# Last quarter of the down projection with the tokens as stationary operand, and the final normalisation along rows

## The reference, cut to what matters

```python
def rmsnorm(x, w):
    xf = x.astype(jnp.float32)
    y = xf * lax.rsqrt(jnp.mean(xf * xf, axis=-1, keepdims=True) + RMS_EPS)
    return (y * w.astype(jnp.float32)).astype(x.dtype)
...
    x = x + mix @ w_out
    hn = rmsnorm(x, ln2_w)
    x = x + jnp.square(jax.nn.relu(hn @ w_up)) @ w_down
```

## Time and profile before

| | |
|---|---|
| median of 3 runs | 700.5 us (700.15 to 701.1) |
| the profiled execution | 700.22 us, span 698.5 us |
| busy: PE, PEld | 683.0 us (98%), 640.9 us (92%) |
| busy: DVE, POOL, ACT | 443.9 us, 323.3 us, 296.3 us |
| DMA | 100.41 MB, mean 144 GB/s |

### The profile page before, as it was taken

One profiled execution on the slowest core, in us unless ns is written; L12 is line 12 of the kernel. 1 busy time (PEld: TensorE's weight loads), 2 busy tenths in 40 slices (PEclk: granted clock), 3 DMA queues, 4 the chain that ended last, 5 costly groups with the idle time before them and its releaser, 6 DMA issues.

```text
span 698.5 us, 15196 instructions
## 1 busy us (share of the span) xinstructions
PE 683.0 (98%) x5563; PEld 640.9 (92%) x5563; DVE 443.9 (64%) x890; ACT 296.3 (42%) x568; POOL 323.3 (46%) x233
## 2 busy tenths in 40 slices
PE   6999999999999999999999999999999999999996
PEld 6999988888777787999999999999999999999996
DVE  4488889886342456537798685857657576575134
ACT  6532735465342233246555443443433534334222
POOL 6839999823131434247327617053260623507431
PEclk9999999999999999999999999999999999999999
DMA  7936999844477888633112323332232331413103
GB/s 246 302 119 168 266 283 276 269 141 119 144 248 205 254 269 183 146 106 122 61 39 84 121 64 126 115 111 78 89 125 80 120 98 66 139 62 121 61 1 123
DMA packets 88633, 100.41 MB, mean 144 GB/s; under 512 B 5374, under 2 KB 64338, under 8 KB 88570
## 3 DMA queue, kind: packets, MB, share of 16 engines
q1 hardware_dynamic: 74566, 92.91, 42.7%
q10 hardware_dynamic: 14004, 6.67, 4.2%
HBM read 92.92 MB, written 6.64 MB: 143 GB/s over the span
## 4 chain that ended last, share of the span: by engine, by line
PE 79%; DVE 9%; POOL 5%; issue 3%; ACT 2%; DMA 1%; SPq 0%; DVEq 0%; POOLq 0%; ACTq 0%
PE acc L915 6%; PE acc L916 6%; PE acc L917 6%; PE acc L1419 5%; PE acc L1420 5%; PE acc L1418 5%; POOL prod L1973 4%; PE scr L1419 3%; PE scr L1420 3%; PE scr L1418 3%; PE scr L1385 3%; PE scr L1384 3%; PE scr L1386 3%; PE acc L1384 3%; PE acc L1386 3%
## 5 line engine op out<-in xcount | busy, mean ns | idle before, releaser
L915 PE MATMUL acc<-act_hi,w_hi 128*128 128x256 f32 (+1 forms) x416 | 120.6, 290 | 0.8 <-DVE zT L2504 0.8
L2020 POOL TENSOR_TENSOR h_lo<-relu,h_hi 128x520 fp32r<-128x520 f32 x32 | 44.2, 1385 | 165.0 <-ACT h_hi L1805 164.6
L916 PE MATMUL acc<-act_lo,w_hi 128*128 128x256 f32 (+1 forms) x416 | 117.3, 282 | 0.0
L917 PE MATMUL acc<-act_hi,w_lo 128*128 128x256 f32 (+1 forms) x416 | 117.2, 282 | 0.0
L1504 POOL TENSOR_TENSOR w_lo<-raw,w_hi 128x1024 fp32r<-128x1024 f32 x24 | 57.2, 2388 | 96.5 <-ACT w_hi L1497 94.1
L1973 POOL TENSOR_TENSOR prod<-kv,Qb 128x1024 f32<-128x1024 f32 x32 | 85.7, 2712 | 15.9 <-DVE S L2206 10.2
L915 PEld LDWEIGHTS acc<-act_hi,w_hi 128*128 128x128 f32 x416 | 78.4, 188 | 3.6 <-issue 2.3
L916 PEld LDWEIGHTS acc<-act_lo,w_hi 128*128 128x128 f32 x416 | 78.4, 189 | 0.5
L917 PEld LDWEIGHTS acc<-act_hi,w_lo 128*128 128x128 f32 x416 | 78.2, 188 | 0.0
L2523 DVE TENSOR_TENSOR xT<-acc,xT 128x260 f32<-128x260 f32 x64 | 26.6, 424 | 48.4 <-PE acc L1420 48.4
L2504 DVE TENSOR_TENSOR zT<-acc,rstd 128x264 f32<-128x264 f32 (+1 forms) x56 | 23.5, 421 | 44.5 <-PE acc L917 41.0
(11 more groups left out here) (422 smaller groups left out, 2302.2 us busy)
## 6 DMA issues: line engine op xcount, KB each, us to landing
kv<-in_cache_k_dram SPq DMA_DIRECT2D x64, 256.0 KB, 3.4
kv<-in_cache_v_dram SPq DMA_DIRECT2D x64, 256.0 KB, 3.0
raw<-in_w_up_dram SPq DMA_DIRECT2D x16, 1024.0 KB, 5.4
raw_d<-in_w_down_dram SPq DMA_DIRECT2D x12, 1024.0 KB, 5.1
raw<-in_w_in_dram SPq DMA_DIRECT2D x14, 512.0 KB, 6.1
raw<-in_w_in_dram SPq DMA_DIRECT2D x7, 1024.0 KB, 7.2
x_tok<-in_x_prompt_dram SPq DMA_DIRECT2D x8, 512.0 KB, 5.4
raw<-in_w_out_dram SPq DMA_DIRECT2D x4, 1024.0 KB, 7.6
```

The costliest lines, as they stand in the source:

```text
L915: pe.matmul(out, W_HI[home(g)][:, k, :], hi[k][:, cols], start=(n == 0), stop=False)
L916: pe.matmul(out, W_HI[home(g)][:, k, :], lo[k][:, cols], start=False, stop=False)
L917: mm = pe.matmul(out, W_LO[home(g)][:, k, :], hi[k][:, cols], start=False, stop=(n == KT - 1))
L2020: pool.tensor_tensor(h_lo[:, t, :], relu2[:, t % 2, :], h_hi[:, t, :].bitcast(F32), ALU.subtract).then_inc(s_hs_lo, 1)
```

## The change

The last quarter is turned round. 128 prompt tokens (`h_hi`, `h_lo`) are the stationary operand, 512 columns of w_down are moving, and the result has tokens on its partitions. There are 16 blocks j: token tile i = j % 4, output half c = j // 4 % 2, hidden eighth d = j // 8. A block is 4 k-tiles of 3 matmuls, 192 matmuls in all. Results go to `y_out` (token rows), no longer to `xT`: for j < 8 ACT copies the block (L1921) and DVE adds the transposed `xT` (`y_to_tok`, 8 groups of 4 transposes, now all of them early in the phase; L2793); for j >= 8 DVE adds the block from PSUM (L2801).

The 8 sample tokens are no longer columns of these matmuls. `down_samples`, once per eighth, multiplies them (`h_smp`, padded to 32 columns) by the unsplit weights in `raw_d`, in float32, spread over four column groups of the array; in the first call eight more products add `xT`. `sample_sums` adds the groups up.

The final normalisation follows each token tile: ACT squares 512 channels and accumulates along the row (L1928), DVE adds the two halves' sums, POOL takes the power, DVE finishes channels 512 to 1023, ACT channels 0 to 511, which POOL has multiplied by lnf_w (L2136). The sample rows go through the same steps, on DVE between token tiles 2 and 3. In the last phase a raw slot's third load also waits for the first `down_samples`. The stores go out in the order 0, 1, samples, 2, 3.

```diff
             counts = [2] * 6 + [1] * 2
         else:
-            counts = [2] * 6 + [0] * 2
+            counts = [2, 2, 0, 0, 0, 0, 2, 2, 2, 2] + [0] * 6
...
+                    if kind == "last" and q >= 2:
+                        sp.wait_ge(s_smp_down, 1)
...
-                        src = w_down[0, e * EIGHTH:, q * 2 * P:(q + 1) * 2 * P]
-                        dst = raw[:, r % 2, :, :]
+                        src = w_down[0, (e + q // 2) * EIGHTH:(e + q // 2 + 1) * EIGHTH,
+                                     (q % 2) * 4 * P:(q % 2 + 1) * 4 * P]
+                        dst = raw_d[:, r % 2, :, :]
...
-            for i in range(NT + 1):
-                sp.wait_ge(s_y_half, i + 1)
-                evacuated(sp, "yt", i, 1)
+            for i in (0, 1, NT, 2, 3):
                 if i < NT:
+                    sp.wait_ge(s_y_half, i + 1)
+                    sp.wait_ge(s_y_fin, i + 1)
                     sp.dma_start(y_prompt[0, i * P:(i + 1) * P, :], y_out[:, i, :]).then_inc(s_y_stored, 16)
                 else:
+                    sp.wait_ge(s_y_fin_s, 1)
...
+            def down_tokens(j):
+
+                i, c, n = j % 4, j // 4 % 2, LAST + 4 * (j // 4)
+                out = acc[:, j % 3, :]
+                if j == 8:
+                    pe.wait_ge(s_hs_lo, 32)
+                bank_free("last", 6, j, 0)
+                for k in range(4):
+                    if i == 0:
+                        lo_made(pe, n + k)
+                    t, tokens = 4 * (j // 8) + k, slice(i * P, (i + 1) * P)
+                    w = flat(u_hi[(n + k) % RING]), flat(u_lo[(n + k) % RING])
+                    pe.matmul(out, h_hi[:, t, tokens], w[0], start=(k == 0), stop=False)
+                    pe.matmul(out, h_lo[:, t, tokens], w[0], start=False, stop=False)
+                    mm = pe.matmul(out, h_hi[:, t, tokens], w[1], start=False, stop=(k == 3))
...
+            def down_samples(d):
...
+                for k in range(4):
+                    for c in range(2):
+                        r = UNITS[LAST + 8 * d + 4 * c][3]
+                        pe.wait_ge(raw_in[r % 2], mlp_raw_target(r))
+                        g = 32 * (2 * c + k % 2)
+                        mm = pe.matmul(acc[g:g + 32, 3, :], h_smp[:, 4 * d + k, :], raw_d[:, r % 2, k, :],
+                                       start=(d == 0 and k < 2), stop=(d == 1 and k >= 2))
...
             def down_last():
...
+                for j in range(16):
+                    down_tokens(j)
...
+                    if 1 <= j < 9:
+                        y_to_tok((j - 1) % 4, (j - 1) // 4)
+                    if j in (3, 11):
+                        down_samples(j // 8)
+                    if j == 13:
+                        sample_sums()
...
+            def down_last():
+
+                squares(7, 3)
+                for j in range(16):
+                    for u in PREPARE["last", 6, j]:
+                        unit_hi(u)
+                    i, c = j % 4, j // 4 % 2
+                    if j < 8:
+                        block_done(act, j)
+                        act.activation(y_half(j), acc[:, j % 3, :], ACT.Copy).then_inc(s_dn_evac, 1)
+                        continue
+                    act.wait_ge(s_dn_evac, 16 * 6 + j + 1)
+                    if j >= 10:
+                        act.wait_ge(s_y_sq, j - 9)
+                    if j == 15:
+                        act.wait_ge(s_y_sq_s, 1)
+                    act.activation(y_junk[:, j % 2, 0:512], y_half(j), ACT.Square, scale=D ** -0.5,
+                                   accum_out=y_sq[:, c, i:i + 1]).then_inc(s_y_sq, 1)
...
+                    if j >= 12:
+                        act.wait_ge(s_y_pow, i + 1)
+                        act.wait_ge(s_y_pre, i + 1)
+                        x = y_out[:, i, 0:512]
+                        act.activation(x, x, ACT.Copy, scale=y_ms[:, i:i + 1]).then_inc(s_y_half, 1)
+                    if j == 14:
...
+                        act.activation(y_junk[0:NS, 1, :], y_out[0:NS, NT, :], ACT.Square, scale=D ** -0.5,
+                                       accum_out=y_sq[0:NS, 0, NT:NT + 1]).then_inc(s_y_sq_s, 1)
...
+            for i in range(NT):
+                pool.wait_ge(s_y_sq, i + 1)
+                x = y_out[:, i, 0:512]
+                pool.tensor_tensor(x, x, lnf_b[:, 0:512], ALU.mult).then_inc(s_y_pre, 1)
+            for i in range(NT):
+                if i == NT - 1:
+                    pool.wait_ge(s_y_ms_s, 1)
+                    rsqrt(y_ms[0:NS, NT:NT + 1], NS, 1).then_inc(s_y_pow_s, 1)
+                pool.wait_ge(s_y_ms_ok, i + 1)
+                rsqrt(y_ms[:, i:i + 1], P, 1).then_inc(s_y_pow, 1)
...
+                for j in range(8, 16):
+                    i, c = j % 4, j // 4 % 2
+                    block_done(dve, j)
+                    evacuated(dve, "yt", i, c)
+                    dve.tensor_tensor(y_half(j), acc[:, j % 3, :], y_half(j), ALU.add).then_inc(s_dn_evac, 1)
...
+                    dve.wait_ge(s_y_eps, i + 1)
+                    dve.wait_ge(s_y_sq, 4 + i + 1)
+                    dve.tensor_tensor(y_ms[:, i:i + 1], y_sq[:, 0, i:i + 1], y_sq[:, 1, i:i + 1], ALU.add)\
+                       .then_inc(s_y_ms_ok, 1)
+                    dve.wait_ge(s_y_pow, i + 1)
+                    dve.scalar_tensor_tensor(out=y_half(j), in0=y_half(j), scalar=y_ms[:, i:i + 1],
+                                             in1=lnf_b[:, 512:D], op0=ALU.mult, op1=ALU.mult).then_inc(s_y_fin, 1)
+                    if i == 1:
+                        out = full(dve, "ys")
+                        for g in range(4):
+                            ins = dve.tensor_copy(y_out[0:NS, NT, 256 * g:256 * g + 256],
+                                                  out[32 * g:32 * g + NS, 0:256]).then_inc(s_y_smp, 1)
+                    if i == 2:
+                        dve.wait_ge(s_y_sq_s, 1)
...
```

More of the change, by code:

```diff
@@ L254, in plan @@
                 job(*name, i)
-    for i in range(NT + 1):
[L256 to L260, removed]
+    for c in range(2):
+        for i in range(NT):
+            job("yt", i, c)
+    job("ys")
     return tasks, jobs
@@ L373, in banks @@
         else:
-            for j in range(16):
-                b = j % 4 if kind == "last" else BANK_ORDER[(6 + j) % 8]
+            for j in range(17 if kind == "last" else 16):
+                b = (j % 3 if j < 16 else 3) if kind == "last" else BANK_ORDER[(6 + j) % 8]
                 use[kind, e, j] = b, last.get(b)
@@ L1333, in _, with y_to_tok @@
                         task(*name)
-            def y_to_tok(i, part):
-                n = P if i < NT else NS
-                out = open_job(pe, "yt", i, part)
+            def y_to_tok(i, c):
+                out = open_job(pe, "yt", i, c)
                 for j in range(4):
[L1340 to L1352, removed]
+                    mm = pe.transpose(out[:, j * P:(j + 1) * P], xT[:, 4 * c + j, i * P:(i + 1) * P], ident[:, :])
                 done(mm)
@@ L1434, in down @@
                                       None if k < 3 else s_u_done if half else s_dn0)
-            def down_last():
[L1438 to L1461, removed]
@@ new lines, in sample_sums @@
+            def sample_sums():
+                pe.wait_ge(s_y_pick, 2)
+                pe.wait_ge(s_y_grp, 1)
+                out = open_job(pe, "ys")
+                for c in range(2):
+                    for q in range(2):
+                        g = 32 * (2 * c + q)
+                        mm = pe.matmul(out[g:g + NS, 0:256], y_pick[:, c, :], y_grp[:, 256 * q:256 * q + 256],
+                                       start=True, stop=True)
+                done(mm)
+            def down_last():
+                for j in range(16):
+                    down_tokens(j)
+                    if j == 1:
+                        pe.wait_ge(s_dn_evac, 16 * 6)
+                        pe.wait_ge(s_c_ok, 14 * 8 - 6)
+                        pe.wait_ge(s_p_copy, 2 * 7)
+                    if 1 <= j < 9:
[4 more added lines that the diff above has]
+                        sample_sums()
@@ L1479, in _ @@
                 phase(what, e)
[L1480 to L1486, removed]
         def weight_hi(act, g, r_slot, target):
@@ L1876, in phase @@
                     up(e, i)
-                else:
[L1878 to L1884, removed]
-                act.activation(y_out[0:n, i, 0:512], y_out[0:n, i, 0:512], ACT.Copy, scale=y_ms[0:n, i:i + 1])\
-                   .then_inc(s_y_half, 1)
+                elif kind == "down":
+                    down(e, i)
+                else:
+                    down_last()
             for s in range(N_HALVES):
@@ L1906, in _ @@
                 phase(what, e)
-            for i in range(NT + 1):
-                y_scale(i)
             act.wait_ge(s_v_out0, 32)
@@ L2043, in phase @@
             def phase(kind, e, i=0):
-                for step in range(14 if kind == "up" else 8):
```

(11 more changed lines are left out.)

149 lines of the change are left out of this document (86 added, 63 removed).

## The result

| | before | after |
|---|---|---|
| median of 6 runs each | 700.37 us (700.15 to 701.1) | 707.2 us (706.61 to 707.79) |
| ratio, 95% interval | | 1.0097 [1.0087, 1.0107] |
| span of the profiled execution | 698.5 | 705.6 |
| start of the phase's first matmul | 640.09 | 640.88 |
| stretch 1, to the start T of the last matmul | 48.9 | 53.2 |

T is the start of the phase's last matmul, as in the prediction. The profiled execution of the changed kernel took 707.74 us. The changed kernel is slower by 6.8 us, where 4.6 were forecast; the time lies in the range. But the two stretches aren't what was forecast: stretch 1 grew by 4.3 (forecast 1.3), stretch 2 by 2.0 (forecast 3.3).

The account below looks back on a forecast made before the run. PE's matmul count times spacing was taken to bound the phase, then a chain across engines after T; +1.3 and +3.3 make +4.6 on 700.22, so 704.8, median 705.1; own range 703.4 to 706.8, stated 702.5 to 707.4.

Parts of the forecast that it names:

- stretch 1: Last phase, first matmul's start to the last one's start T: 48.9 us before, forecast 50.2, so 1.3 longer.
- stretch 2: From T to the end of the span, the tail: 9.5 us before, forecast 12.8, so 3.3 longer.
- Rival 1: Tail: DVE does not pile up, last add starts at T + 0.4, end at T + 7.4; 699.7 us, chance 0.14.
- eight float32 products in four column groups, 1.0 us from start to start: PE in stretch 1: price of one down_samples call; with 0.1 for the switch, 2.2 us for two calls.
- the other two terms: PE in stretch 1: eight products with `xT` in four groups, 0.3 us, and sample_sums, 0.3 us.
- Rival 3: Stretch 1: 512-column matmuls near the bare 2.4 GHz rate, 0.216 us each; 702.9 us, chance 0.05.
- Rival 4: Sample products on PE: column groups do not overlap, adding 4.8 us; 709.9 us, chance 0.03.
- rival 2: PE stalls 1 to 2 us at block 8 for weight unit 10 or 11; 706 to 707 us, chance 0.10.
- The store: End of the tail: last store's issue to the span's end, taken as 3.7 us, lower bound 3.0.
- The add of block 15: DVE in the tail: the last block's add starts at T + 5.8 instead of T + 0.4, behind the samples.
- the four copies: DVE after tile 1: four 8x256 sample copies out of PSUM, about 0.35 us each back to back, 1.4 us.
- the samples' chain: Tail after tile 2: ACT's sample square, DVE, POOL and DVE's 8x1024 multiply ahead of the last add; 3.9 us.

Follow-up runs that it names:

- experiment 5: Changed kernel with block 15's add moved in DVE's order to right behind tile 2's multiply, ahead of the samples' mean and multiply: 706.37 us, ratio 1.0084.
- experiment 6: Changed kernel with the tail's order on DVE, ACT and POOL rewritten and the samples' sums on PE put earlier, no work left out: 702.28 us, ratio 1.0026.
- experiment 1: Changed kernel without the samples' work in the last phase, y_sample stored as zeros: 697.5 us, ratio 0.995.
- Experiment 2: Changed kernel without the products of k-tiles 2 and 3 in both down_samples calls (8 of 16): 705.47 us, ratio 1.0067.
- experiment 3: Changed kernel with sample products in two column groups instead of four, sample_sums and ACT's copy gone, DVE copying 2 x 512 columns: 710.51 us, ratio 1.0141.
- experiment 4: Changed kernel with each 512-wide matmul of the 16 blocks split into two of 256 columns: 707.75 us, ratio 1.010.

## Why the prediction was right, and where it was wrong

**The direction and its mechanism held.** What was removed, the 9.5 us behind T, is gone as a whole, and what took its place is, as said, DVE waiting in its own order with the last add behind the samples. Of the points of the changed profile that were named, these came true: the spacing of 0.23, the last add right behind the samples' multiply (T + 5.33), ACT's sample square between the scalings of tiles 2 and 3, the last store alone, no idle PE ahead of block 8; the 50.2 and 12.8 us of the two stretches did not. Experiments 5 and 6 show the cause by moving only the order. Rival 1 (DVE does not pile up) is what experiment 6 produces; there the order that it needs had to be written.

**The step that failed: "eight float32 products in four column groups, 1.0 us from start to start".** The row was counted as products where it counts two records for each. The loop behind the earlier trace rows in the kernel before issues four products a time; eight records to four products should have been seen by dividing. Measured: from the end of block 3's transposes (653.38) to one spacing ahead of 656.09, 2.5 us with the `xT` products; 2.1 for the second call and 0.75 for the sums, each with the longer first spacing behind it: 5.3 where 2.8 stood in the sum (5.4 by experiment 1). The same doubling is in the other two terms: L1491 has 16 records for eight products and takes 0.55, where 0.3 were forecast. Experiment 2 shows the size (1.84 us for half of the products), experiment 3 excludes the other explanation.

**The rest of stretch 1.** 191 spacings of 0.2325 are 44.4, forecast 44.0: +0.4. Transposes 3.5 as forecast. 44.4 + 3.5 + 5.3 = 53.2. Rival 3, 0.216 per matmul, would have made them 41.3; neither this trace nor experiment 4 agrees. The Trainium skill (TensorE: Matmul & The Clock Gate, Back-to-back issue gap) gives this 0.216 as the gap of a single matmul with 512 columns; for a stream of weight loads and matmuls the same section has 0.131, which this stream, at 0.2325, is further from still. Rival 4 is excluded by experiment 3, rival 2 by the unchanged spacing around block 8.

**The tail was forecast 1.3 too long.** The store 3.0 where 3.7 was taken, though 3.0 was the lower bound: -0.7. Its bytes start to move 0.83 after the issue (the prediction had 0.4 for this as a bound that no run shows), move for 1.44, and the span ends 0.8 later. The add of block 15 at T + 5.33, not 5.8: block 12's add came 0.5 earlier against T, since the sums stand between it and T and take more, and the chains are shorter, 3.04 for a tile and not 3.11 (-0.2 in all); the four copies took 1.8, not 1.4, 0.45 each (+0.4); the samples' chain 3.8, forecast 3.9. From add to issue 3.2, forecast 3.3.

**So the two errors partly cancel**: +3.0 in stretch 1, -1.3 in the tail. That the time fell within the range is in part luck. It lies outside the 703.4 to 706.8 that the forecast's own terms gave, and inside the stated 702.5 to 707.4 only because this was widened for rival 2, a stall of PE at block 8 that did not occur. The remaining 0.4 between 705.1 + 1.7 and 707.2 lies outside the span: each of the changed kernel's six runs took 2.1 us more than its span, where the kernel before took 1.7 to 1.8 in all 24 runs beside the experiments. The prediction had carried the 1.7 over. Experiments 1 and 3, which have no `sample_sums`, are at 1.7 to 1.8 again, all others at 2.0 to 2.1; what makes the difference was not tried. The start of the phase is another matter and belongs to single executions: its first matmul, with only unchanged work ahead of it, starts at 640.09 before, 640.88 after, and between 639.82 and 641.26 in the experiments, which is why the profiled spans differ by 7.1 us and the stretches by 6.3.

## What to carry to other kernels

Before a row of the trace becomes the price of an operation, divide its count by what the code issues: here a float32 product leaves two records, a transpose one, and each of the three matmuls on split fp32r operands one. When a few odd rows (8 of 520) are taken out of wide matmuls where they were 4 of 260 columns, price them as an operation of their own, in every engine; here they cost 9.7 us, three times the 3.2 by which the changed kernel without them was ahead. And in a tail in which several engines hand one tile round, write each engine's list so that the next tile's first step stands in front of the wait for this tile's last one: by order alone 4.9 us of 707 came back.

## What the hardware showed that I had not expected

- A float32 product with 512 moving columns leaves two records, about 0.43 us from one to the next; in four column groups of 32, four products start 7 ns apart, and all four take no longer than two in two groups (the changed kernel and experiments 2 and 3).
- The spacing of these fp32r matmuls, 256 to 512 columns wide, is 0.447 ns per column and 3.5 ns for the matmul, at a granted clock of 1.00 (before, changed kernel and experiment 4).
- From the issue of the last store of 0.5 MB to the end of the span it is 3.0 us where the store before was issued 2.7 us earlier, and 3.3 where a like one was issued 1.1 us earlier (experiments 5 and 6): there the bytes of the two stores move without a pause between them and end at 703.45 in experiment 5, 0.3 later than 0.83 + 1.44 after the last issue.
- The time that an execution takes outside its span is not the same for all of these kernels: 1.7 to 1.8 us in the kernel before and in experiments 1 and 3, 2.0 to 2.1 in the others, in every run.
